# Splitting the gated projection and gates of a hybrid decoder layer into high and low parts, with x kept in DRAM meanwhile

## The chip, the core and the metric

The kernel runs on one core of a Trainium2 chip. The metric is the time of one execution in device microseconds (us). A core has five engines with a queue of instructions each: TensorE (PE, matrix products), VectorE (DVE), ScalarE (ACT), GpSimd (POOL) and SyncE (SP, which here only starts transfers). They meet only through semaphores: an instruction waits for a count, and another one raises it when it is done.

## The reference, cut to what matters

One layer for two groups of tokens that share the weights: 512 prompt tokens and 64 sample tokens (8 sequences of 8), 1024 channels wide.

```python
x = x + 0.5 * swiglu_ffn(rms_norm(x, g_ffn1), w_ffn1_in, w_ffn1_out)
h = rms_norm(x, g_mix)
a_glu, b_glu, q, k, v, qi, ki, wi, gc, ga = split(h @ w_in)
u = a_glu * sigmoid(b_glu)                       # gated projection
q, k = rope(rms_norm(q, g_q)), rope(rms_norm(k, g_k))
scores = sum_h wi * relu(qi . ki);  idx = top_k(scores)   # keys per query
att = softmax(q . k[idx] / 8) @ v[idx]
conv = silu(layer_norm(depthwise_conv31(u))) @ w_cout
x = x + (sigmoid(gc) * conv + sigmoid(ga) * (att @ w_aout)) @ w_o
x = x + 0.5 * swiglu_ffn(rms_norm(x, g_ffn2), w_ffn2_in, w_ffn2_out)
```

Sample tokens gather 256 keys and values each from paged caches of 4096 tokens; prompt tokens attend to keys of the prompt under a mask. q, k, v and the indexer's columns are the "native" part of `h @ w_in`; a_glu, b_glu (512 columns each) and the gates gc, ga (1024 each) are the gated projection and the gates.

## The kernel before

Everything of one token lies in one column: x (`xT`), h (`h32`) and the gates are tiles of 128 channels by 576 tokens (64 sample, 512 prompt), eight of them for 1024 channels. A matmul takes a 128x128 piece of weights and half of the tokens (288).

The program is written out by hand, engine by engine, in the order in which each runs it. In time the stages are: the sample path, the first FFN and the index scores to about 600 us; the native projection to 723.6; `mix_unit` n = 0 to 13 (L1079), PE's gated projection (n = 0 to 7) and the first gate units, to about 869; 32 steps of prompt attention (four blocks of 128 queries times eight heads), into which PE weaves `gate_half`, halves of the units n = 14 to 23 (L1198, in the steps of `HALF_AT`); from `conv_sums` (L1241, about 1063) the norm of the convolution, the output projections (`unit`, L592) and the second FFN.

**Two ways to multiply.** A *fp32 unit* is a weight tile of 128 x 4 x 256 (512 KB) times four tiles of h: 16 matmuls of type fp32, which the profile records as 32 PE records. A *split unit* has its weight in `w_raw` (two slots), from which ACT copies the high part into `w_hi` (L1303, type fp32r) and POOL or DVE subtracts it for the low part `w_lo` (L2651, L1812, L1856); then PE does three products per tile, high by high, high by low, low by high: 48 records. Before, n = 0 to 23 are fp32 units, with weights in a ring of six slots, `wn`, which lies on the place of `w_raw`, `w_hi` and `w_lo`. The output units UM and following are split ones.

**What runs beside.** DVE: `key_logits` (L2356 product, L2359 reduction), one per sample token, 64 in all, 15 of them ("late keys") after the prompt scores; `prompt_qk(0)` and `(1)` (squares, root on ACT, scale, gain, rope) for q and k of the prompt; `u_pair(0)`, `(1)` (gate times projection; they wait for units 3 and 7); the sample softmax over L (64x2560: add bias L2472, maximum L2477, subtract L2478, ACT's Exp L1610, sum L2481, multiply L2483); `choose(b, from, to)`, rounds of eight maxima (L2439, L2440) that pick the prompt's keys per block; `own_heads(0)` (L2508), which waits for PE's first eight value groups. In step i it makes the mask (L2495), four convolution taps (L2530) and the quotient (L2501). POOL gathers key rows (`gather`, L2707, two instructions a token), after the last key clears `zq` and gathers value rows (`gather_values(j)`, L2719, four instructions, 32 groups in three buffers), which PE multiplies in `values(j)` (L1094). SP sends query rows (L476) between weight loads. PE's `logits_turn` (L1113) follows unit 4 and waits for the last key; `probs_turn` (L1121) waits for the normalised L. x stays in `xT`, 2.4 MB, which the final parts read.

## Time and profile before

| | |
|---|---|
| median of 3 runs | 1585.39 us (1580.94 to 1587.18) |
| profiled execution, its own time | 1588.44 us |
| its span in the trace | 1586.6 us |
| PE busy | 1484.6 us, 94% |
| DVE busy | 1104.5 us, 70% |
| POOL busy | 585.4 us, 37% |
| ACT busy | 499.6 us, 31% |

Busy is the time in which an instruction runs; a wait in a queue isn't. "Idle before" in a row names what the instruction was seen to wait for: "issue" is nothing that the profile shows, "remote" something outside of the engines. All times below are from the start of the span.

### The profile page before, as it was taken

To read this page: it belongs to the slowest core of one execution; us is meant where nothing else is said; L and a number is where in the kernel's file an instruction comes from. 1 tells how busy PE (TensorE), PEld (TensorE's weight loads), DVE (VectorE), ACT (ScalarE), POOL (GpSimd) and SP (SyncE) were. 2 spreads that over 40 slices of the span, in tenths; PEclk is the share of its full clock that TensorE was granted. 3 is DMA by queue.
4 is the path that set the end of the run, shared out by engine and by line. 5 is a ranking of instruction groups with operands and counts; after the bars stand their busy time and mean duration, and the time that the engine had idled before them with its cause. 6 is when DMAs were issued, how large, how long until landed. Compare 5 with 4: busy or idle time off the path is not lost. (4 is left out here: it accounts for less than half of the span.)

```text
span 1586.6 us, 20793 instructions
## 1 busy us (share of the span) xinstructions
PE 1484.6 (94%) x8219; PEld 1147.5 (72%) x8219; DVE 1104.5 (70%) x1680; ACT 499.6 (31%) x756; POOL 585.4 (37%) x412
## 2 busy tenths in 40 slices
PE   5989999899999989999899789999999999999998
PEld 2323488677888865446666445669999999999998
DVE  1357399999985898999996676565679865565221
ACT  2233322112112222121212344464346544453221
POOL 2001264443338865554245775013120645520000
PEclk9998999999999999999999898999999999999999
DMA  9994153222226888868458776023422332222222
GB/s 343 389 381 161 50 85 113 93 80 80 80 80 221 286 276 276 290 213 278 125 163 269 222 237 187 17 101 126 138 75 68 93 107 82 92 68 74 74 87 93
DMA packets 156931, 248.77 MB, mean 157 GB/s; under 512 B 11965, under 2 KB 104909, under 8 KB 156571
## 3 DMA queue, kind: packets, MB, share of 16 engines
q1 hardware_dynamic: 131742, 164.22, 32.0%
q0 software_dynamic: 23104, 76.16, 15.4%
q10 hardware_dynamic: 1989, 7.07, 1.1%
q8 instruction: 64, 1.05, 0.3%
q14 instruction: 32, 0.26, 0.0%
HBM read 237.58 MB, written 10.20 MB: 156 GB/s over the span
## 5 line engine op out<-in xcount | busy, mean ns | idle before, releaser
L2651 POOL TENSOR_TENSOR w_lo<-w_raw,w_hi 128x1024 fp32r<-128x1024 f32 x65 | 165.5, 2546 | 294.8 <-ACT w_hi L1303 294.6
L686 PE MATMUL ps<-bh,wqr 128*128 128x288 f32 x936 | 205.3, 295 | 4.2 <-DVE wqr L1843 2.0
L1303 ACT ACTIVATE w_hi<-w_raw 128x1024 fp32r<-128x1024 f32 x88 | 91.5, 1040 | 314.7 <-PE ps L637 231.5
L2707 POOL DMA_INDIRECT kv<-cache_k,idxT x128 | 142.2, 1111 | 81.4 <-DVE kprod L2356 48.9
L2719 POOL DMA_INDIRECT kv<-cache_v,idxT x128 | 134.7, 1052 | 99.3 <-PE ps L1094 47.0
L686 PEld LDWEIGHTS ps<-bh,wqr 128*128 128x128 f32 x936 | 155.5, 188 | 5.0 <-DVE wqr L1843 3.9
L637 PE MATMUL ps<-h_hi,w_hi 128*128 128x512 f32 x352 | 139.2, 395 | 2.8 <-POOL w_lo L2651 1.5
L637 PE MATMUL ps<-h_lo,w_hi 128*128 128x512 f32 x352 | 137.7, 391 | 0.0
L637 PE MATMUL ps<-h_hi,w_lo 128*128 128x512 f32 x352 | 137.7, 391 | 0.0
L1079 PE MATMUL ps<-h,wn 128*128 128x288 f32 x448 | 115.5, 417 | 8.1 <-ACT sgb L1587 4.6
L702 PE MATMUL ps<-a_hi,wqr 128*128 128x288 f32 x704 | 122.3, 295 | 0.0
L686 PE MATMUL ps<-bl,wqr 128*128 128x288 f32 x384 | 113.3, 295 | 0.0
L1079 PEld LDWEIGHTS ps<-h,wn 128*128 128x128 f32 x448 | 86.2, 195 | 37.0 <-ACT sgb L1587 6.2
L1044 PE MATMUL ps<-wn,xg 128*128 128x512 f32 (+1 forms) x256 | 103.2, 563 | 5.0 <-DVE xT L2175 3.0
L702 PEld LDWEIGHTS ps<-a_hi,wqr 128*128 128x128 f32 x704 | 103.1, 188 | 0.0
L1856 DVE TENSOR_TENSOR wqr<-wq,wqr 128x1024 fp32r<-128x1024 f32 (+1 forms) x24 | 27.2, 1135 | 95.2 <-ACT wqr L1341 95.2
L1044 PEld LDWEIGHTS ps<-wn,xg 128*128 128x128 f32 x256 | 49.7, 196 | 56.2 <-issue 47.1
L1198 PE MATMUL ps<-h,wn 128*128 128x288 f32 x320 | 88.3, 432 | 0.7 <-ACT sgb L1686 0.7
L2356 DVE TENSOR_TENSOR kprod<-kv,qb 128x1024 f32<-128x1024 f32 x64 | 81.9, 1280 | 8.5 <-issue 3.1
L2775 POOL TENSOR_TENSOR wq<-wq 128x1024 f32<-128x1024 f32 x10 | 24.9, 2490 | 170.4 <-PE ps L686 76.7
L637 PE MATMUL ps<-a1h,w_hi 128*128 128x512 f32 x176 | 71.6, 407 | 14.8 <-DVE w_lo L1812 7.5
L1198 PEld LDWEIGHTS ps<-h,wn 128*128 128x128 f32 x320 | 62.6, 201 | 27.2 <-issue 8.7
(493 smaller groups left out, 3268.9 us busy)
## 6 DMA issues: line engine op xcount, KB each, us to landing
w_raw<-w_ffn_in SPq DMA_DIRECT2D x56, 512.0 KB, 13.1
wq<-w_ffn_in SPq DMA_DIRECT2D x40, 512.0 KB, 3.6
wn<-w_in SPq DMA_DIRECT2D x36, 512.0 KB
qb<-q_scratch SPq DMA_DIRECT2D x64, 256.0 KB
ring<-w_ffn_in SPq DMA_DIRECT2D x28, 512.0 KB
w_raw<-w_ffn_out SPq DMA_DIRECT2D x24, 512.0 KB, 10.1
wq<-w_ffn_out SPq DMA_DIRECT2D x20, 512.0 KB
ring<-w_ffn_out SPq DMA_DIRECT2D x14, 512.0 KB
```

What stands on the lines that cost most here:

```text
L637: mm = pe.matmul(ps[:, 2 * half + m, :], w[:, k, m * P:(m + 1) * P], x[:, kc0 + k, c0:c0 + SEQ], start=(first and k == 0 and fst), stop=(l ...
L686: mm = pe.matmul(ps[:, bank + m, 0:HALF], w[:, k, m * P:(m + 1) * P], b[:, j, k, :], start=(j in (0, 1, 5) and k == 0 and fst), stop=(k == ...
L702: mm = pe.matmul(ps[:, 4 * half + 2 * m + hf_, 0:HALF], w[:, k, m * P:(m + 1) * P], x[:, kc0 + k, hf_ * HALF:(hf_ + 1) * HALF], start=(kc0 ...
L1044: mm = pe.matmul(ps[:, s % 8, 0:n], xg[:, kk, P * b:P * b + P], wt[:, k, :], start=(kk == 0), stop=(kk == KD - 1))
L1079: mm = pe.matmul(ps[:, 4 * half + 2 * m + hf_, 0:HALF], wt[:, k, m * P:(m + 1) * P], h32[:, 4 * (n % 2) + k, hf_ * HALF:(hf_ + 1) * HALF], ...
L1198: mm = pe.matmul(ps[:, 2 * m + hf_, 0:HALF], wt[:, k, m * P:(m + 1) * P], h32[:, 4 * (n % 2) + k, hf_ * HALF:(hf_ + 1) * HALF], start=(n % ...
L1303: act.activation(w_hi[:, slot, 0:n], w_raw[:, slot, 0:n], ACT.Copy).then_inc(S_("hi_ready"), 1)
L1856: dve.tensor_tensor(wqr[:, 6 + o % 2, 0:n], wq[:, 8 + o % 2, 0:n], wqr[:, 4 + o % 2, 0:n].bitcast(F32), ALU.subtract).then_inc(S_("lo_read ...
L2356: dve.tensor_tensor(kprod[:, :, :], kv[:, n % KV, :, :], qb[:, j, :].unsqueeze(1).to_broadcast([P, 2, DA]), ALU.mult)\
L2651: pool.tensor_tensor(w_lo[:, slot, 0:n], w_raw[:, slot, 0:n], w_hi[:, slot, 0:n].bitcast(F32), ALU.subtract)\
L2707: pool.indirect_dma_start(kv[:, n % KV, c, :], None, rows[0], bass.IndirectOffsetOnAxis(ap=idxT[:, c, n:n + 1], axis=0))\
L2719: pool.indirect_dma_start(kv[:, V_SLOT[j % 3] + a // 2, a % 2, :], None, rows[1], bass.IndirectOffsetOnAxis(ap=idxT[:, j % 2, t:t + 1], ax ...
```

## The change

- All 24 units n = 0 to 23 (now UA + n) become split units, with `x_hi` (eight ACT copies of h, in the place of `xT`) and `h_lo` (eight DVE subtractions ahead of the late keys). ACT makes all high parts; the low parts are made by POOL for n = 0 to 9 and 11, by DVE (`gate_lo`) for 10, 12 to 15 and, in the steps of `HI_AT` (one step later), for 16 to 23.
- x goes to DRAM (`x_scratch`, eight stores by SP at native loads 6 to 8) and comes back, two transfers ahead of each of the loads UM + 4 to UM + 7; DVE waits for it before the first update.
- Raw tiles UA, UA + 1 are loaded once 11 and 14 native loads are used up; the last query rows are sent behind the loads of UA to UA + 3.
- DVE has less to do: the squares of `prompt_qk` are made by ACT (Square over 128x2048) and reduced in one instruction; rope has six instructions and not seven; the subtraction and the sum of the softmax are gone, ACT's Exp is eight instructions with a bias and an accumulated sum; `choose(1, 7, 16)` and `choose(2, 0, 2)` follow `u_pair(1)`.
- `probs_turn` follows unit 7, the stores of k and v are waited for at gate unit 6 and not 10, and SP, ACT and POOL lose waits for `ring_used` ahead of UM's loads.

```diff
-        UM = UA
+        UM = UA + 24
+        HI_AT = {3: 16, 5: 17, 9: 18, 11: 19, 15: 20, 17: 21, 21: 22, 25: 23}
...
+                if m < NB + 2:
+                    sp.wait_ge(S_("ring_used"), N_RING + (11, 14)[m - NB])
+                load(UA + m - NB, win_v[:, 4 * (m % 2):4 * (m % 2) + 4, col:col + 256], m % 2, 1024)
+                while m < NB + 4 and sent[0] < (55, 57, 60, NS)[m - NB]:
+                    query_load(sent[0])
+                    sent[0] += 1
...
+                unit(UA + n, n % 2, x_hi, h_lo, 4 * (n % 2), 4, half, n % 2 == 0, n % 2 == 1, between)
...
-                if n == 6:
+                if n == 7:
                     probs_turn()
...
+                    act.wait_ge(S_("nat_evac"), 8)
+                    act.activation(qk_sq[:, :, :], qn[:, :, :], ACT.Square).then_inc(S_("nat_squares"), 1)
                     for j in range(3):
                         relu(8 * j, 8 * j + 8)
+                        if j < 2:
+                            act.wait_ge(S_("x_moved"), 64 + 16 * KD)
+                            for k in range(4 * j, 4 * j + 4):
+                                act.wait_ge(S_("hf_ready"), KD + k + 1)
+                                act.activation(x_hi[:, k, :], h32[:, k, :], ACT.Copy).then_inc(S_("hhi_ready"), 1)
...
-            act.activation(L[:, :, :], L[:, :, :], ACT.Exp, scale=HD ** -0.5).then_inc(S_("exp_ready"), 1)
+            for h in range(H):
+                act.activation(L[:, h, :], L[:, h, :], ACT.Exp, scale=HD ** -0.5, bias=small[0:NS, 40 + h:41 + h],
+                               accum_out=small[0:NS, 50 + h:51 + h]).then_inc(S_("exp_ready"), 1)
...
+            for k in range(KD):
+                dve.wait_ge(S_("hhi_ready"), KD + 1 + k + 1)
+                dve.tensor_tensor(h_lo[:, k, :], h32[:, k, :], x_hi[:, k, :].bitcast(F32), ALU.subtract).then_inc(S_("h_ready"), 1)
...
+            def gate_lo(n):
+
+                dve.wait_ge(S_("lo_ready"), UA + n + 2)
+                split_lo(UA + n, n % 2)
...
             while sent[0] < NS:
+                if sent[0] == 56:
+                    pool.wait_ge(S_("ring_used"), N_RING + 13)
+                    lo(UA)
+                if sent[0] == 62:
+                    pool.wait_ge(S_("ring_used"), N_RING + NB)
+                    lo(UA + 1)
                 gather()
+            lo(UA + 2)
             pool.wait_ge(S_("logits_ready"), NS + 1)
             pool.memset(zq[:, :, :, :], 0.0).then_inc(S_("zq_zero"), 1)
-            pool.wait_ge(S_("ring_used"), N_RING + NB + 3)
-            for j in range(3):
-                gather_values(j)
+            gather_values(0)
+            lo(UA + 3)
+            lo(UA + 4)
+            gather_values(1)
+            lo(UA + 5)
+            gather_values(2)
+            lo(UA + 6)
             pool.wait_ge(S_("shift_ready"), 1)
             pool.memset(zq2[:, :, :, :], 0.0).then_inc(S_("zq_zero"), 1)
+            for n in range(7, 10):
+                lo(UA + n)
             for j in range(3, 32):
+                if j == 5:
+                    pool.wait_ge(S_("lo_ready"), UA + 11 + 2)
+                    lo(UA + 11)
                 gather_values(j)
```

The order on POOL around the last key (kv is the buffer of gathered rows). Before:

```order
L2707 DMA kv<-cache_k,idxT 128x512 [waits kv_used]
L2707 DMA kv<-cache_k,idxT 128x512
L2744 MEMSET zq 128x448 [waits logits_ready]
L2719 DMA kv<-cache_v,idxT 128x512 [waits kv_used,ring_used]
L2719 DMA kv<-cache_v,idxT 128x512 x3
L2719 DMA kv<-cache_v,idxT 128x512 [waits kv_used]
L2719 DMA kv<-cache_v,idxT 128x512 x3
```

And now, from the split of unit 1 on:

```order
L2705 TENSOR_TENSOR w_lo<-w_raw,w_hi 128x1024 [waits hi_ready,ring_used]
L2761 DMA kv<-cache_k,idxT 128x512 [waits kv_used]
L2761 DMA kv<-cache_k,idxT 128x512
L2761 DMA kv<-cache_k,idxT 128x512 [waits kv_used]
L2761 DMA kv<-cache_k,idxT 128x512
L2705 TENSOR_TENSOR w_lo<-w_raw,w_hi 128x1024 [waits hi_ready]
L2805 MEMSET zq 128x448 [waits logits_ready]
L2773 DMA kv<-cache_v,idxT 128x512 [waits kv_used]
L2773 DMA kv<-cache_v,idxT 128x512 x3
L2705 TENSOR_TENSOR w_lo<-w_raw,w_hi 128x1024 [waits hi_ready] x2
L2773 DMA kv<-cache_v,idxT 128x512 [waits kv_used]
L2773 DMA kv<-cache_v,idxT 128x512 x3
```

The splits of units 0 and 1 stand among the last key gathers, that of unit 2 ahead of the wait for the last key (logits_ready), those of units 3 and 4 behind the first group of values.

On DVE, the end of the sample softmax (L is the tile of logits, sgb the sigmoid, m_192 and m_194 the eight maxima of a round of `choose`). Before:

```order
L2439 MAX m_192<-bias_new 128x8 [waits dve_own]
L2440 MATCH_REPLACE bias_new<-m_192,bias_new 128x256 [waits dve_own]
L2481 TENSOR_REDUCE small<-L 64x8 [waits exp_ready,dve_own]
L2482 RECIPROCAL small<-small 64x8 [waits dve_own]
L2483 TENSOR_TENSOR L<-L,small 64x2560 [waits dve_own]
L2439 MAX m_192<-bias_new 128x8 [waits dve_own]
L2440 MATCH_REPLACE bias_new<-m_192,bias_new 128x256 [waits dve_own]
```

And now:

```order
L2474 MAX m_194<-bias_new 128x8 [waits dve_own]
L2475 MATCH_REPLACE bias_new<-m_194,bias_new 128x256 [waits dve_own]
L2520 RECIPROCAL small<-small 64x8 [waits exp_ready,dve_own]
L2521 TENSOR_TENSOR L<-L,small 64x2560 [waits dve_own]
L2220 TENSOR_TENSOR U_s<-sgb,ps 128x8x8 [waits unit_used,mix_free,sgb_ready]
L2222 TENSOR_TENSOR U_p<-sgb,ps 128x224
L2223 TENSOR_TENSOR U_p<-sgb,ps 128x288
```

The sum is gone, and `u_pair(1)` (L2220 to L2223) has moved ahead of the rounds that stood behind the product.

On DVE, a step of the prompt attention (Lp the masked logits, yacc the convolution's sum). Before:

```order
L2495 ISA Lp,small<-ps,causal 128x128 [waits plog_done]
L2495 ISA small 128x1
L2530 SCALAR_TENSOR_TENSOR yacc<-U_p,wconv,yacc 128x512 [waits dve_own]
L2530 SCALAR_TENSOR_TENSOR yacc<-U_p,wconv,yacc 128x512 x3
L2501 RECIPROCAL small<-small 128x1 [waits pexp_ready]
```

And now, in a step that follows one of `HI_AT`:

```order
L2541 ISA Lp,small<-ps,causal 128x128 [waits plog_done]
L2541 ISA small 128x1
L2580 SCALAR_TENSOR_TENSOR yacc<-U_p,wconv,yacc 128x512 [waits dve_own]
L2580 SCALAR_TENSOR_TENSOR yacc<-U_p,wconv,yacc 128x512 x3
L1849 TENSOR_TENSOR w_lo<-w_raw,w_hi 128x1024 [waits hi_ready,lo_ready]
L2547 RECIPROCAL small<-small 128x1 [waits exp_ready]
```

A split stands between the taps and the quotient, with a wait for ACT's high part.

## Rows read from the trace of the kernel before

**Rows 1.** Windows: us, busy of PE, PEld, DVE, ACT, POOL, clock, DMA.
```profile
724.00:798.00 74.00, 67.84 (x298) 52.55 (x297) 69.09 (x106) 13.88 (x17) 19.53 (x17) 0.98 0.54 168
798.00:869.00 71.00, 66.14 (x329) 43.42 (x327) 54.35 (x100) 14.40 (x32) 36.78 (x37) 0.98 0.70 220
869.00:998.00 129.00, 113.32 (x527) 64.78 (x527) 88.26 (x175) 50.09 (x119) 82.40 (x80) 0.92 0.68 208
844.30:850.00 5.70, 5.69 (x16) 4.02 (x16) 0.00 (x0) 1.28 (x3) 2.89 (x4) 0.70 0.97 332
```

**Rows 2.** Timeline of DVE: start, us, line, operation, count, idle before.
```profile
740.00 1.22 DVE L2359 TENSOR_REDUCE G<-kprod 128x16 f32<-128x1024 f32 x1
...
781.46 2.82 DVE L2483 TENSOR_TENSOR L<-L,small 64x2560 f32<-64x2560 f32 x1
...
795.86 0.22 DVE L2185 TENSOR_TENSOR U_s<-sgb,ps 128x64 f32<-128x64 f32 x1
...
797.57 1.22 DVE L2081 TENSOR_TENSOR rt<-kn 128x1024 f32<-128x1024 f32 x1
...
851.24 0.69 DVE L2508 TENSOR_TENSOR mz<-ps,headmask 128x512 f32<-128x512 f32 x1 [13.97 <-issue]
...
873.46 0.27 DVE L2495 CUSTOM_DVE_ANT_0 Lp<-ps,causal 128x128 f32<-128x128 f32 x1
```

**Rows 3.** Timeline of PE, late units and the first steps.
```profile
821.78 4.15 PE L1079 MATMUL ps<-h,wn 128*128 128x288 f32 x16
...
844.31 5.81 PE L1079 MATMUL ps<-h,wn 128*128 128x288 f32 x16 [2.99 <-ACT sgb L1587]
...
874.39 0.49 PE L1213 MATMUL ps<-kTp,qTp 64*128 64x128 f32 x2
877.75 1.32 PE L1094 MATMUL ps<-kv,zq 128*32 128x512 f32 x8 [2.87 <-issue]
```

**Rows 4.** Timeline of PE, fp32 units, the logits' turn, and a split unit.
```profile
723.64 14.71 PE L1079 MATMUL ps<-h,wn 128*128 128x288 f32 x60
...
762.44 1.91 PE L1113 MATMUL ps<-ident,G 128*64 128x128 f32 x16
...
1067.72 0.53 PE L592 MATMUL ps<-t_hi,w_hi 128*128 128x288 f32 x2 [0.16 <-DVE t_lo L2582]
...
1074.17 4.04 PE L1241 MATMUL ps<-ysq,ones 128*128 128x288 f32 x16
```

**Rows 5.** Groups by line, DVE from 1063 to 1068 us (busy, mean ns).
```profile
L2582 DVE TENSOR_TENSOR t_lo<-attT,t_hi 128x576 fp32r<-128x576 f32 x4 | 2.8, 752 | 6.2 <-ACT t_hi L1742 6.2
```

**Rows 6.** Timeline of ACT at the native projection and the softmax.
```profile
718.69 0.69 ACT L1583 ACTIVATE vnp<-ps,small 128x512 f32<-128x512 f32 x1 [16.61 <-issue]
...
774.65 2.34 ACT L1610 ACTIVATE L<-L 64x2560 f32<-64x2560 f32 x1
```

**Rows 7.** Timelines of POOL and of DVE at an earlier POOL split.
```profile
496.20 2.40 POOL L2651 TENSOR_TENSOR w_lo<-w_raw,w_hi 128x1024 fp32r<-128x1024 f32 x1
...
496.63 3.04 DVE L2356 TENSOR_TENSOR kprod<-kv,qb 128x1024 f32<-128x1024 f32 x1
```

**Rows 8.** Timeline of POOL after the last key.
```profile
741.28 0.47 POOL L2744 MEMSET zq<- 128x448 f32 x1 [13.56 <-DVE G L2359]
747.36 3.00 POOL L2719 DMA_INDIRECT kv<-cache_v,idxT  x1 [5.60 <-PE ps L1079]
750.66 2.01 POOL L2719 DMA_INDIRECT kv<-cache_v,idxT  x1 [0.30 <-issue]
752.98 0.95 POOL L2719 DMA_INDIRECT kv<-cache_v,idxT  x1 [0.30 <-issue]
```

**Rows 9.** The page's groups of instructions: busy, mean ns, idle before.
```profile
L1303 ACT ACTIVATE w_hi<-w_raw 128x1024 fp32r<-128x1024 f32 x88 | 91.5, 1040 | 314.7 <-PE ps L637 231.5
...
L702 PEld LDWEIGHTS ps<-a_hi,wqr 128*128 128x128 f32 x704 | 103.1, 188 | 0.0
L1856 DVE TENSOR_TENSOR wqr<-wq,wqr 128x1024 fp32r<-128x1024 f32 (+1 forms) x24 | 27.2, 1135 | 95.2 <-ACT wqr L1341 95.2
```

145 lines of the change are left out of this document (86 added, 59 removed).

## The prediction

> **What bounds the kernel now.** I read the table of windows first, then the timelines of DVE and PE, and last POOL's. [rows 1] is that table. From 724 to 869 us PE is busy for 134 of 145 us, DVE for 123; from 869 to 998 us, where the prompt attention runs in steps, PE has 113.3 and DVE 88.3 of 129. So PE leads by little, and DVE is second. The timelines show where the two take turns: DVE ends the last key of the sample logits at 741.2, works on `prompt_qk`, softmax and `choose`, waits 13.97 us for PE's sparse values up to 851.24, and makes its first prompt mask at 873.46 [rows 2]; PE comes to step 1 at 874.39, so both reach the steps together [rows 3]. Whatever either engine is given or spared before 873 counts only by what the later one of the two does. After the steps nothing of the program changes but the reload of x; that stretch (from `conv_sums` on) I move as a block.
>
> **What the split saves on PE.** A gated unit is 32 fp32 records: 14.71 us for 60 of them is 0.245 each, 7.8 us a unit. The same tile shape in high and low parts is 48 records; those of the first output unit start at 1067.72 and the next thing starts at 1074.17: 6.45 us [rows 4]. That is 1.36 us a unit, 0.68 a half, and 33 us for the 24 units if all of it were on the path.
>
> **What is added ahead of the first unit.** DVE makes h_lo, eight subtractions of 128x576, between the prompt scores and the last fifteen keys. Four such keep DVE busy for 2.8 us [rows 5], so 5.5 us. ACT's first Square of 128x2048 and its eight x_hi copies stand ahead of relus whose scores DVE waits for; an Exp of 2560 columns took ACT 2.34 us [rows 6], so the Square takes about 1.9. What of this DVE feels the trace can't show; I take 1.0, with ends 0 (ACT has idle time) and 3. Then POOL's splits of units 0 to 2 run beside the keys. The trace shows what that costs: while POOL split from 496.20 to 498.60, DVE's product of keys took 3.04 us and not 1.22, ending where it would if it had begun when the split ended [rows 7]. The next two such collisions cost less, since a split may begin under the reduction, which is not held up. I take 1.2 each, 3.7 for three (ends 0 and 7). The Trainium skill, "SBUF — State Buffer", section "SBUF: two separate sides", says that VectorE's operation with two SBUF inputs and a GpSimd operation reading SBUF exclude each other for the whole instruction; by it the POOL splits are no free cover, and without it the sum would be about 4.5 us lower. The trace agrees. Last key: 741.2 + 5.5 + 1.0 + 3.7 = **751.4**.
>
> **The new wait.** Splits of units 0 to 2 stand ahead of POOL's wait for the last key, but the split of unit 3 stands behind it, behind a memset (0.47) and behind `gather_values(0)`. Before, the first two gathers of values took 3.00 and 2.01 us beside DVE's 2048-wide products, the later ones 0.95 with 0.30 between [rows 8]: 8.1 us for the four, 5.0 without such neighbours. A split takes 2.4 [rows 7], and may stand behind one more DVE product: 751.4 + 0.5 + 8.3 + 0.8 + 2.4 = 763.4. PE began unit 0 at 723.64 [rows 4]; 1.0 later and with three units of 6.45 it is free at 744. It **waits about 19 us** for unit 3. All of PE's saving up to here and 15 us more is gone; behind the wait stand units 3 to 7, the logits' turn, and by these DVE's softmax and `u_pair(1)`. After 2.99 us of idleness a half took 5.81 instead of 4.15 us [rows 3, 4], in a window with a granted clock of 0.70 [rows 1], that is, part of it at the lower level of 1.2 GHz; I add 1.7. Five units at 6.45, the turn (1.9 [rows 4]) and 1.7 make 35.9: PE ends unit 7 at 799.3, and `u_pair(1)`, 1.7 us from 795.86 to 797.57 [rows 2], ends at **801.0** where it ended at 797.57. DVE's removed work (two passes over L of 2.8 us each, and the first `prompt_qk`'s squares) lies in this stretch. It buys nothing, since DVE waits for unit 7 anyway; nor does the longer Exp on ACT cost anything: 2.34 us in eight pieces [rows 6], say 6 with what each piece adds, against the 12 us that PE still needs for units 6 and 7.
>
> **DVE from there to the first mask.** Before: 873.46 − 797.57 = 75.9, less the wait of 13.97 and 0.3: 61.6 of work. Added: the `choose` rounds that stood between 784.28 and 795.86 and now follow `u_pair(1)`, 11.6 [rows 2]; five `gate_lo` of 1.14 [rows 9], 5.7. Taken off in `prompt_qk(1)`: squares in four passes of 1.22 [rows 2] become one reduction over 2048, about 2.2, and the copy of rope goes, 0.7: 3.4. Sum 75.5. The wait of 13.97 is filled: DVE now comes to `own_heads(0)` at about 850, when PE, with units of 6.45 us, has the eighth value group. `gate_lo(13)` waits for an ACT split that waits for unit 11, 2.3 us; one more POOL split (11) collides, 0.5. First mask at 801.0 + 75.5 + 2.8 = 879.3, **+5.8**. PE is through its units at 860 and idles.
>
> **Steps.** Step 1 loses its wait of 2.87 us for a V gather [rows 3], since POOL has had time to run ahead; half of it returns as DVE's own chain there: −1.4. From step 2 on PE is the longer engine: thirteen halves × 0.68 = −8.8; DVE's six `gate_lo` there make a step DVE-bound now and then: +0.6. Steps 21 to 34: six halves, −4.1, and +0.7 for the last two `gate_lo`. Together −8.2 and −3.4. POOL's five us for a value group stay below the steps' 5.6.
>
> The tail is unmoved: x goes out behind native loads while the DMA share is high but nobody waits for these eight, and comes back over 50 us before the first use.
>
> **Sum:** +5.8 − 1.4 − 8.2 − 3.4 = **−7.2**. The profiled run of before took 1588.44, so its like would be 1581.2; the median of the three shown is 1585.39, so **1578.2**. A measurement of this kernel can tell about 0.5%, 7.9 us, from no change; this lies just inside.
>
> **Rivals.**
> (1) *The wait at unit 3 is shorter or is absorbed.* If gathers and splits meet no DVE products, unit 3 starts at 751.4 + 0.5 + 5.0 + 2.4 = 759.3 and without slow restart: 5.8 less, so −13.0, 1572.4. If moreover the keys are not held up, 3.7 less: 1568.7. The end of this side is DVE without any wait: before, DVE took 56.4 us from the last key to the end of `u_pair(1)`, of which it waited about 1.9; without 9.0 of removed work and 11.6 of moved rounds 33.9 are left, and 78.3 behind: 863.6, −9.9 instead of +5.8: 1562.5. For it: the gathers' 0.95 rows; against it: [rows 7, 8].
> (2) *Slower: the chain within a step binds, not PE's sum.* A mask on DVE, exp on ACT, quotient on DVE, scale on ACT, turn on PE. ACT is busy for 50 and DVE for 88 us of the 129 [rows 1], and they wait for each other. Then shorter halves buy nothing, and each step with a split adds 1.04 on ACT and 1.14 on DVE [rows 9]: eight × 2.2 = +17.6 in place of −11.6. With +5.8 − 1.4 it gives +22, 1607; where only half of the steps are so, +7.4, 1592.8. It decides from the point where DVE's and ACT's work of one step exceeds PE's 5.6 us. Against it: PE's 113 of the same 129 us.
> (3) *The split gives nothing.* Each record needs a weight load of 0.188 [rows 9]; were these not hidden, a unit would be 9.0 us. Against it stand the 6.45 us of rows 4. +29 and more: 1614.
> (4) *Gathers 56 to 63 come late*, behind the splits of units 0 and 1 on POOL: the last key moves one for one once the split of unit 0 ends after 721. ACT, which makes the high parts, idled 16.61 us before 718.69 [rows 6], so this is unlikely; I give it no more than a part of the slower chance, at 1586 to 1594.
>
> **Chances.** Forecast, −7.9 to +7.9: 0.44. Rival 1, beyond −7.9: 0.41. Rivals 2 and 4, beyond +7.9: 0.12; rival 3: 0.03. Faster 0.41, same 0.44, slower 0.15. The range of 8 in 10 takes rival 1 to its end, and of rival 2 the half: 1562.5 to 1592. The forecast's own range is 1572 to 1586.
>
> **What would show it.** PE's unit 3 starts at 763 after a wait of 15 to 20 us put down to POOL's w_lo; if it starts before 755 the POOL reasoning is wrong. 48 records a unit in 6.45 us. DVE's key product near a POOL split at 2 to 3 us. The first mask at 876 to 882, with PE idle for over 10 us before it. Steps from first mask to `conv_sums` 12 to 14 us shorter. If instead DVE's idle time in steps shrinks and PE's grows, rival 2 holds. Wrong altogether: waits for x or for query rows in the profile.

## The result, and the profile after

| | before | after |
|---|---|---|
| median of nine runs each, first chip | 1585.39 us | 1591.68 us |
| ratio, 95% interval | | 1.0038 [1.0019, 1.0056] |
| profiled execution, its span | 1586.6 us | 1589.6 us |
| PE busy | 1484.6 us | 1456.8 us |
| DVE busy | 1104.5 us | 1123.6 us |
| POOL busy | 585.4 us | 624.2 us |

The change made the kernel slower by 6.3 us of median, which is small but outside of the interval. Two more comparisons on other chips gave 1.0051 [1.0032, 1.0071] and 1.0066 [1.0044, 1.0087]. The forecast had been 7.2 us faster; the time lies 0.3 us inside the upper end of the range. PE lost 27.8 us of work, of the 33 that the prediction gave for all 24 units, and none of it reached the end.

Where the time went, as distances between marks that both traces have (c0 is one more trace of the kernel before, c1 and c2 are two more of the kernel after, on other chips; c0 and c1 share one):

| us | before | c0 | after | c1 | c2 | forecast for after |
|---|---|---|---|---|---|---|
| end of the last key | 741.2 | 743.6 | 756.0 | 755.5 | 757.4 | 751.4 |
| end of `u_pair(1)` | 797.6 | 799.9 | 806.5 | 805.8 | 807.1 | 801.0 |
| first prompt mask | 873.5 | 875.8 | 891.0 | 894.2 | 893.0 | 879.3 |
| first mask to that of step 20 | 118.6 | 118.7 | 110.4 | 109.7 | 108.3 | 109.0 |
| mask of step 20 to `conv_sums` | 71.3 | 71.1 | 64.9 | 67.9 | 67.7 | 67.9 |
| `conv_sums` | 1063.4 | 1065.6 | 1066.3 | 1071.8 | 1069.1 | 1056.2 |
| from there to the end of the span | 523.2 | 524.2 | 523.3 | 523.9 | 523.2 | unmoved |

So the steps shortened just as forecast, and the first mask came 12 us later than forecast. Read like this, the failure would lie wholly ahead of the first mask. The experiments speak against this reading: where the first mask came early, the steps did not shorten.

These marks come from one profiled execution each. That of the kernel before took 1588.44 us, 3 us more than its median, so in the first pair `conv_sums` moved by only 2.9 us, and by 6.2 from c0 to c1.

Windows of the kernel after, against [rows 1] (us, busy of PE, PEld, DVE, ACT, POOL with counts, clock, DMA share, GB/s):

```profile
724.00:869.00 145.00, 116.61 (x825) 103.08 (x824) 122.36 (x174) 45.73 (x78) 95.61 (x70) 0.91 0.63 200
869.00:998.00 129.00, 103.36 (x624) 69.13 (x624) 107.69 (x205) 56.51 (x124) 88.62 (x83) 0.88 0.71 216
998.00:1061.00 63.00, 60.79 (x383) 45.35 (x382) 45.97 (x91) 35.84 (x67) 2.39 (x1) 0.95 0.18 62
```

In the middle window PE fell by 10.0 us against [rows 1], DVE rose by 19.4 and POOL by 6.2: the three longest now have 103, 108 and 89 of 129. POOL's number leaves out the 0.30 us for which it is idle after each gather, about 80 times in that window; with them POOL is taken for some 113 of the 129 us.

Timeline of the kernel after on DVE, from the low parts of h to the first mask (start, us, line, operation, idle before):

```profile
706.23 5.43 DVE L2500 TENSOR_TENSOR h_lo<-h,x_hi 128x576 fp32r<-128x576 f32 x8
...
716.80 2.90 DVE L2391 TENSOR_TENSOR kprod<-kv,qb 128x1024 f32<-128x1024 f32 x1
...
736.77 1.91 DVE L2391 TENSOR_TENSOR kprod<-kv,qb 128x1024 f32<-128x1024 f32 x1
...
743.55 3.34 DVE L2391 TENSOR_TENSOR kprod<-kv,qb 128x1024 f32<-128x1024 f32 x1 [1.00 <-DMA qb<-q_scratch]
...
754.76 1.22 DVE L2394 TENSOR_REDUCE G<-kprod 128x16 f32<-128x1024 f32 x1
...
784.06 3.11 DVE L2510 COPY L<-nlog 64x512 f32<-64x512 f32 x1 [3.50 <-PE ps L1119]
...
828.19 3.41 DVE L2097 TENSOR_TENSOR rt<-kn,ropetp 128x1024 f32<-128x1024 f32 x1
...
848.98 1.26 DVE L1849 TENSOR_TENSOR w_lo<-w_raw,w_hi 128x1024 fp32r<-128x1024 f32 x1 [3.76 <-ACT w_hi L1311]
...
864.08 1.23 DVE L1849 TENSOR_TENSOR w_lo<-w_raw,w_hi 128x1024 fp32r<-128x1024 f32 x1 [2.91 <-issue]
...
891.00 0.28 DVE L2541 CUSTOM_DVE_ANT_0 Lp<-ps,causal 128x128 f32<-128x128 f32 x1
```

The eight subtractions took 5.43 us, forecast 5.5. A key product beside a POOL split took 2.90, 1.91 and 3.34 us. The last reduction ends at 755.98.

The new wait, on POOL's timeline of the kernel after:

```profile
743.40 2.40 POOL L2705 TENSOR_TENSOR w_lo<-w_raw,w_hi 128x1024 fp32r<-128x1024 f32 x1
...
756.04 0.47 POOL L2805 MEMSET zq<- 128x448 f32 x1 [10.24 <-DVE G L2394]
...
759.19 2.99 POOL L2773 DMA_INDIRECT kv<-cache_v,idxT  x1 [0.30 <-issue]
...
764.53 5.93 POOL L2705 TENSOR_TENSOR w_lo<-w_raw,w_hi 128x1024 fp32r<-128x1024 f32 x2
```

and on PE's:

```profile
767.20 0.85 PE L608 MATMUL ps<-x_hi,w_hi 128*128 128x288 f32 x2 [14.64 <-POOL w_lo L2705]
...
782.04 1.91 PE L1119 MATMUL ps<-ident,G 128*64 128x128 f32 x16
```

PE waits 14.64 us for the split of unit 3, put down to POOL's `w_lo` as forecast; the forecast had 19 us, since it let PE begin unit 0 at 724.6, and PE began it at 728.2 and waited 2.62 us for the split of unit 1. Windows of the kernel after (columns as above), of unit 8 and then of the two units behind the wait:

```profile
806.50:813.10 6.60, 6.58 (x49) 6.41 (x49) 6.15 (x21) 3.92 (x6) 2.06 (x1) 1.00 0.34 101
```

```profile
767.20:774.90 7.70, 7.70 (x43) 7.70 (x44) 7.63 (x5) 0.00 (x0) 6.94 (x4) 0.71 0.65 182
774.90:782.00 7.10, 7.10 (x55) 7.10 (x54) 4.75 (x17) 1.06 (x1) 6.25 (x5) 1.00 0.71 206
```

The first row is unit 8: 48 records of it, and one more, in 6.6 us with the granted clock at 1.00, forecast 6.45 for a unit. After 14.64 us of idleness the clock is 0.71 for 7.7 us, part of it at 1.2 GHz, and 43 records fill them, where the next 7.1 us at 1.00 hold 55.

### The profile page after: what moved, and what is told of

It reads as the page before. It is cut to its first block and busy times, and to the rows that moved or that the text cites. A ratio compares the mean times of both kernels' runs of the same rounds, so it can differ in the third digit from the quotient of the medians.

```text
span 1589.6 us, 21713 instructions
## 1 busy us (share of the span) xinstructions
PE 1456.8 (92%) x8603; PEld 1162.9 (73%) x8603; DVE 1123.6 (71%) x1687; ACT 533.9 (34%) x805; POOL 624.2 (39%) x423
## 5 line engine op out<-in xcount | busy, mean ns | idle before, releaser
L2705 POOL TENSOR_TENSOR w_lo<-w_raw,w_hi 128x1024 fp32r<-128x1024 f32 x76 | 194.6, 2561 | 294.1 <-ACT w_hi L1311 293.8
L1311 ACT ACTIVATE w_hi<-w_raw 128x1024 fp32r<-128x1024 f32 x112 | 116.9, 1044 | 367.7 <-PE ps L653 235.3
L2773 POOL DMA_INDIRECT kv<-cache_v,idxT x128 | 142.7, 1114 | 62.5 <-issue 35.0
L2391 DVE TENSOR_TENSOR kprod<-kv,qb 128x1024 f32<-128x1024 f32 x64 | 86.6, 1353 | 13.7 <-DMA qb<-q_scratch 5.8
L653 PE MATMUL ps<-a1h,w_hi 128*128 128x512 f32 x176 | 71.1, 404 | 15.3 <-DVE w_lo L1849 8.0
L2580 DVE SCALAR_TENSOR_TENSOR yacc<-U_p,wconv,yacc 128x512 f32<-128x512 f32 x116 | 81.4, 763 | 0.0
L1880 DVE TENSOR_TENSOR wqr<-wq,wqr 128x1024 fp32r<-128x1024 f32 x47 | 74.8, 1604 | 7.8 <-ACT wqr L1334 6.0
L653 PEld LDWEIGHTS ps<-h_hi,w_hi 128*128 128x128 f32 x352 | 66.7, 189 | 18.0 <-issue 2.1
L2394 DVE TENSOR_REDUCE G<-kprod 128x16 f32<-128x1024 f32 x64 | 78.2, 1222 | 2.2
```

Of the source, the lines that this page charges most:

```text
L653: mm = pe.matmul(ps[:, 2 * half + m, :], w[:, k, m * P:(m + 1) * P], x[:, kc0 + k, c0:c0 + SEQ], start=(first and k == 0 and fst), stop=(l ...
L1311: act.activation(w_hi[:, slot, 0:n], w_raw[:, slot, 0:n], ACT.Copy).then_inc(S_("hi_ready"), 1)
L1880: dve.tensor_tensor(wqr[:, s, :], wq[:, s, :], left_hi(i, j).bitcast(F32), ALU.subtract).then_inc(S_("lo_ready"), 1)
L2391: dve.tensor_tensor(kprod[:, :, :], kv[:, n % KV, :, :], qb[:, j, :].unsqueeze(1).to_broadcast([P, 2, DA]), ALU.mult)\
L2394: dve.tensor_reduce(G[:, :, n], kprod[:, :, :].rearrange("p c (h d) -> p (c h) d", h=H), AX.X, ALU.add).then_inc(S_("logits_ready"), 1)
L2580: link(dve.scalar_tensor_tensor(out=yacc[:, k, NS:NT], in0=U_p[:, k, j:j + SEQ], scalar=wj, in1=yacc[:, k, NS:NT], op0=ALU.mult, op1=ALU.add))
```

## Experiments

Ratios are to the kernel before on the same chip. Chips differ: the kernel before had a median of 1568 to 1588 us on them, so times of different groups of runs are compared as ratios only. The kernel after had 1.0038, 1.0051 and 1.0066 on the three chips on which it ran unchanged; a difference of 0.2% between ratios from two chips says nothing.

### Group 1: the parts ahead of the first mask

The four ran on one chip, and the kernel after didn't run there unchanged.

**DVE's savings alone**, in the kernel before:

```diff
-            act.activation(L[:, :, :], L[:, :, :], ACT.Exp, scale=HD ** -0.5).then_inc(S_("exp_ready"), 1)
+            for h in range(H):
+                act.activation(L[:, h, :], L[:, h, :], ACT.Exp, scale=HD ** -0.5, bias=small[0:NS, 40 + h:41 + h],
+                               accum_out=small[0:NS, 50 + h:51 + h]).then_inc(S_("exp_ready"), 1)
...
-                qk_squares(v, rt1[:, :, :, :].rearrange("p b h d -> p (b h) d"), msq, rt2[:, 0, 0:1, :].rearrange("p a b -> p (a b)"))\
-                    .then_inc(S_("ms_ready"), 1)
+                lk(dve.tensor_reduce(msq, qk_sq[:, :, :].rearrange("p b (h d) -> p (b h) d", d=HD), AX.X, ALU.add))
```

> The kernel before with only the savings on VectorE: squares by ACT and one reduction, six rope instructions, no subtraction and no sum in the sample softmax, eight Exp with bias and accumulated sum. The places of choose and u_pair stay. Chain theory: of the 12.6 us removed from DVE only what stands between the logits' turn and the probabilities' turn is on the path, since PE is waited for elsewhere (the 13.97 us before 851.24): probabilities' turn 3 us earlier (784.3 to 781), first mask 3 us earlier, the whole 3 us faster, about 1582.4. Rival, DVE binds from the last key to the first mask: 10 to 12 us faster, about 1574. Second rival, it comes to nothing because ACT's Square delays the scores: 0.

1.0008 [0.9994, 1.0022]. The savings are worth nothing alone, as the prediction said of the softmax part ("it buys nothing, since DVE waits for unit 7 anyway"). The first mask stands at 869.9, `conv_sums` at 1047.0. Since its time is that of before, this trace serves below as the one of before for this chip; its profiled execution took 1571.48 us, 3.4 more than the median of the kernel before there.

**The split of unit 3 ahead of POOL's wait for the last key**, in the kernel after:

```diff
             lo(UA + 2)
+            lo(UA + 3)
             pool.wait_ge(S_("logits_ready"), NS + 1)
...
             gather_values(0)
-            lo(UA + 3)
             lo(UA + 4)
```

> The changed kernel with one line moved: POOL makes the low part of unit 3 before it waits for the last key, not after it and behind the first group of values. Chain theory (last key, POOL, unit 3, units 4 to 7, u_pair(1), first mask): unit 3 starts at 752 to 756 and not at 767.2; the last key comes 2 us later because one more key product is held up by a POOL split; the logits' turn, now waiting for u_pair(0), comes at 777 and not at 782; first mask and end 5 us earlier than in the changed kernel, about 1587. Rival, DVE's own work between last key and first mask binds and the wait of PE at unit 3 only shows idle time: 0 to 2 us, about 1591.

1.0052 [1.0033, 1.0071]. PE's timeline in that kernel:

```profile
766.09 0.82 PE L608 MATMUL ps<-x_hi,w_hi 128*128 128x288 f32 x2 [9.46 <-POOL w_lo L2705]
```

The wait has only moved on: unit 3 starts in time, unit 4 now waits 9.46 us for a split that stands behind the gathers. The logits' turn came at 774.4, the first mask at 882.5, `conv_sums` at 1050.5, and the ratio is among those of the kernel after.

**No subtraction on POOL** (w_lo of all gated units that POOL splits is filled with zeros by a memset):

```diff
-                split_lo(u, u % 2, usize(u))
+                if UA <= u < UM:
+                    pool.wait_ge(S_("hi_ready"), u + 1)
+                    pool.memset(w_lo[:, u % 2, :].bitcast(F32), 0.0).then_inc(S_("lo_ready"), 1)
+                else:
+                    split_lo(u, u % 2, usize(u))
```

> The changed kernel in which POOL's low parts of the gated units are set to zero by a memset in place of the subtraction (the low parts of 11 units are left out; same semaphores). A memset reads nothing from SBUF. Lock theory (a POOL subtraction holds up DVE's products): no key product over 1.3 us, last key 4.5 us earlier (756 to 751.5), rope instructions and the copy of new logits back at 1.2 and 0.4 us, unit 3 about 7 us earlier, first mask 10 us earlier (891 to 881), time about 1582. Rival, POOL's own duration is what counts and DVE isn't held up by it: only the 1.3 us less for the split of unit 3, 2 us in all, about 1590.

1.0016 [1.0001, 1.0031]. DVE's groups by line between the scores and the last key, first of the kernel after (704 to 757 us), then of this one (704 to 760), each with busy, mean ns of one, and idle before:

```profile
L2391 DVE TENSOR_TENSOR kprod<-kv,qb 128x1024 f32<-128x1024 f32 x16 | 24.1, 1503 | 2.7 <-DMA qb<-q_scratch 1.0
```

```profile
L2391 DVE TENSOR_TENSOR kprod<-kv,qb 128x1024 f32<-128x1024 f32 x15 | 18.4, 1225 | 2.3 <-DMA qb<-q_scratch 0.5
```

With a memset in its place the split costs DVE nothing: products take 1.225 us, not 1.503. The last key ended at 749.3 and the first mask came at 879.4, which is 11.6 us ahead of the kernel after on the first chip; `conv_sums`, at 1045.3, was ahead of the stand-in for before (1047.0), and the median still 0.16% behind. The edit relieves POOL, too: a memset takes it 0.97 us and a split 2.4. That matters further down, where POOL's gathers of values come up.

**Short h_lo** (16 of 576 columns subtracted, x_hi in its place in the products):

```diff
-                dve.tensor_tensor(h_lo[:, k, :], h32[:, k, :], x_hi[:, k, :].bitcast(F32), ALU.subtract).then_inc(S_("h_ready"), 1)
+                dve.tensor_tensor(h_lo[:, k, 0:16], h32[:, k, 0:16], x_hi[:, k, 0:16].bitcast(F32), ALU.subtract).then_inc(S_("h_ready"), 1)
```

> The changed kernel in which DVE subtracts only 16 of 576 columns for each of the eight h_lo tiles and PE takes the high part of h in its place (the product of high weights and low h is left out in value, not in work). Chain theory: the 5.4 us come off one for one: last key 751, first mask 886, end 5 us earlier, about 1587. Rival, something else is late at the keys (query rows, gathers, POOL): the last key moves by less than 2.5 us and so does the end.

1.0056 [1.0037, 1.0076]; last key at 752.4, first mask at 885.4, `conv_sums` at 1051.5. Taking 4.6 us off DVE there didn't show in the time.

What follows from the four: the early split and the short h_lo leave the ratio where the kernel after has it, though each takes some us off the way to the first mask. Only the memset brought something, 5.0 us of median against the short h_lo, with a first mask 6.1 us earlier. This alone would fit a first mask that counts one for one. But its gathers moved as well: the last gather of values ends at 980.2 for 986.4, as much earlier as `conv_sums` (1045.3 for 1051.5). Which of the two counts, the next groups tell.

### Group 2: the steps, with the first mask early

**Nine rounds of choose(3) moved into the steps** (nobody needs them before step 24), so that the first mask is no longer late:

```diff
+        CHOOSE_AT = (0, 2, 8, 14, 17, 19, 20, 21, 22)
...
-            choose(3, 6, 16)
+            choose(3, 6, 7)
...
+                if i in CHOOSE_AT:
+                    r = 7 + CHOOSE_AT.index(i)
+                    choose(3, r, r + 1)
```

> The changed kernel with nine of the sixteen rounds of choose for the last block of queries (1.52 us each on DVE) moved from ahead of the first mask into steps 0, 2, 8, 14, 17 and 19 to 22, of which none has a low part or, up to 16, a sample convolution. The block's mask is first needed in step 24. Theory, DVE's work binds the first mask while PE idles 13 us before it: first mask 13 us earlier, steps 21 to 24 a little longer, end 8 to 11 us earlier than in the changed kernel. Rival, PE's late units bind the steps and DVE's lateness costs only idle time: 0 to 3 us. Second rival, the steps' chains take it back: first mask 13 us earlier, conv_sums within 3 us of the changed kernel.

1.0055 [1.0036, 1.0074], against 1.0051 [1.0032, 1.0071] of the kernel after, unchanged, on the same chip:

> The changed kernel, unchanged, on the chip of the next two. Expected by the first comparison: 0.2 to 0.6% slower than before. If the wait at unit 3 and the first mask (17 us late in the first pair) are the same here while the 13 to 15 us won in the steps shrink, as the steps of the experiments above suggest (177 and 168 us), it is 0.6 to 0.9% slower.

and the kernel before:

> The kernel before, unchanged, for a trace from the same chip as the next three. The chain of after is compared against it mark by mark. Expected: last key at about 741, first mask 873, conv_sums at the place of the first trace or up to 15 us earlier, since the kernels of the first group of experiments ran 17 us faster on their chip than the kernels on the first one.

The masks of steps 0 and 20 on DVE, in c0, c1 and this kernel:

```profile
875.83 0.28 DVE L2495 CUSTOM_DVE_ANT_0 Lp<-ps,causal 128x128 f32<-128x128 f32 x1
...
994.50 0.54 DVE L2495 CUSTOM_DVE_ANT_0 Lp<-ps,bias_new 128x384 f32<-128x384 f32 x1
```

```profile
894.20 0.28 DVE L2541 CUSTOM_DVE_ANT_0 Lp<-ps,causal 128x128 f32<-128x128 f32 x1
...
1003.94 0.54 DVE L2541 CUSTOM_DVE_ANT_0 Lp<-ps,bias_new 128x384 f32<-128x384 f32 x1
```

```profile
877.20 0.29 DVE L2542 CUSTOM_DVE_ANT_0 Lp<-ps,causal 128x128 f32<-128x128 f32 x1 [0.23 <-DVE bias_new L2476]
...
996.86 0.56 DVE L2542 CUSTOM_DVE_ANT_0 Lp<-ps,bias_new 128x384 f32<-128x384 f32 x1
```

The first mask came 17.0 us earlier and the mask of step 20 only 7.1. From the one to the other it took 118.7, 109.7 and 119.7 us. Six of the nine rounds lie between these two masks and bring DVE 8.7 us (96.5 us busy for 87.9 in c1), into a stretch in which DVE had waited for others. So with the first mask in its old place the steps take as long as before, though their halves are split: the shortening of 8 to 10 us in the steps of the kernel after was not won by the split units. By this run alone it could be the moved rounds that took it back, if DVE paced the steps; the run with half of the taps, in the next group, speaks against that.

PE in this kernel waits early in the steps for nothing that the profile names, ahead of the products of gathered values:

```profile
884.09 1.93 PE L1101 MATMUL ps<-kv,zq 128*32 128x512 f32 x8 [6.04 <-issue]
```

**All known losses mended** (the former, with the split of unit 3 early, ACT's first Square behind the relus, and `gate_lo(13)`, `(14)` three rounds later):

```diff
+            lo(UA + 3)
             pool.wait_ge(S_("logits_ready"), NS + 1)
...
-            choose(2, 2, 8)
+            choose(2, 2, 11)
             gate_lo(13)
-            choose(2, 8, 16)
+            choose(2, 11, 16)
             own_heads(0)
+            choose(3, 0, 3)
             gate_lo(14)
```

> The same with three things more: unit 3's low part ahead of the wait for the last key, ACT's first Square behind the relus of the prompt scores, and the low parts of units 13 and 14 three rounds of choose later, where the trace of the changed kernel shows DVE waiting 3.8 and 2.9 us for ACT's high part. Chain theory: to the 10 us of the run before come 5 for unit 3, 2 for the Square, up to 5 for the waits, of which PE's own late units will swallow half: 14 to 18 us faster than the changed kernel, 7 to 12 us faster than before. Rival: no more than 3 us beyond the run before, since PE, not DVE, then binds the start of the steps.

1.0050 [1.0031, 1.0069]: first mask at 875.0, before the one of c0, `conv_sums` at 1067.5, still 1.9 us behind it. So a first mask in time, 0.9 us ahead of c0's, does not bring the time of before back.

### Group 3: which engine paces the steps

Three engines came into question for steps 2 to 20: PE, DVE with the masks and taps, and POOL with four gathers of values per group. Each was relieved alone. ACT, with its part of the softmax in each step, was not.

This group ran on a chip as quick as that of group 1 (a median of 1569 and 1568 us for the kernel before), and its base, the kernel with moved rounds, wasn't traced there. From the first mask to that of step 20 the stand-in for before took 105.9 us in group 1, where the kernel before took 118.6 and 118.7 on slower chips. The distances below must be set beside each other and beside that 105.9, and not beside the 119.7 of group 2.

**Half of the gathers from group 15 on** (the former with moved rounds as base; two of four gathers left out):

```diff
+                    if j >= 15 and a == 1:
+                        break
```

> The kernel with nine rounds of choose in the steps (first mask early, no gain at the end), in which POOL issues only two of the four value gathers of each group from the 15th on (the other two quarters of those groups are left out, PE multiplies what the buffer held). Theory A, POOL's gathers pace steps 2 to 20: from the first mask to the 20th 119.7 us become about 100, the end 12 to 20 us earlier, 0.990 to 0.995 of before. Theory B, the chain mask, Exp, quotient, scale, turn through DVE, ACT and PE paces the steps: less than 4 us.

The counts that PE waits for are lowered to match. 1.0038 [1.0020, 1.0055], for 1.0055 of its base on another chip; masks at 879.1 and 982.9, 103.9 apart, in the slowest of its nine executions. POOL now waits for PE, here at its last gathers:

```profile
961.96 0.94 POOL L2777 DMA_INDIRECT kv<-cache_v,idxT  x1 [3.38 <-PE ps L1101]
963.21 0.95 POOL L2777 DMA_INDIRECT kv<-cache_v,idxT  x1 [0.30 <-issue]
967.97 0.95 POOL L2777 DMA_INDIRECT kv<-cache_v,idxT  x1 [3.82 <-PE ps L1101]
```

**Half of the convolution's taps on DVE** (same base):

```diff
-                for k in range(KC):
+                for k in range(KC if j in (0, CW - 1) else 2):
```

> The same kernel as its base, in which DVE makes the taps of the convolution for two of four channel tiles only (half of that work is left out): 1.4 us less of DVE in every step. Theory B, DVE's part of the chain paces the steps: steps 2 to 20 shorter by 1.0 to 1.4 us each, 20 us or more, and steps 21 to 31 as well. Theory A, POOL's gathers: DVE gives way, but the gathers still come at 6 us a group: less than 6 us up to step 20.

1.0063 [1.0044, 1.0083], from four runs; masks at 873.9 and 982.2, 108.3 apart. DVE is busy for 73.4 us between them, less than the 80.7 of the kernel before, and the steps are no shorter for it. So it isn't DVE's moved rounds that keep the steps long. In the table of waits from 880 to 998 us (engine, line waited for, us in total, times, longest) DVE now waits for PE's scores:

```profile
DVE Lp L2542 <- PE ps L1222: 31.5, 14, 4.6
```

**Half of the matmuls in the gate halves, kernel before** (38 us of PE's work gone):

```diff
-                for k in range(4):
+                for k in range(2):
...
-                                       start=(n % 2 == 0 and k == 0), stop=(n % 2 == 1 and k == 3))
+                                       start=(n % 2 == 0 and k == 0), stop=(n % 2 == 1 and k == 1))
```

> The kernel before, in which PE does only half of the matmuls of each gate half in the steps (the other half of the channels is left out): 2 us less of PE in each of 20 steps, three times what the split saves. My prediction held PE for the longer engine there: then the 13 halves of steps 2 to 20 give 26 us and the six later ones 12, the time about 0.977 of before. Rival, PE's time is cover and gathers or the softmax chain pace the steps: less than 8 us in steps 2 to 20, 0.99 or more.

0.9926 [0.9903, 0.9948]: 12 to 13 us won for 38 removed. Its table of waits from 880 to 998 us:

```profile
PE ps L1094 <- DMA kv<-cache_v,idxT: 16.3, 9, 3.6
```

and its last gather of values on POOL, and the mask of step 20 on DVE:

```profile
969.07 0.95 POOL L2719 DMA_INDIRECT kv<-cache_v,idxT  x1 [0.30 <-issue]
```

```profile
971.78 0.53 DVE L2495 CUSTOM_DVE_ANT_0 Lp<-ps,bias_new 128x384 f32<-128x384 f32 x1
```

The windows from the first mask to that of step 20 (columns as above), of the stand-in for before and then of this kernel:

```profile
869.92:975.85 105.93, 99.06 (x479) 56.82 (x479) 80.67 (x160) 48.11 (x113) 80.57 (x76) 0.95 0.76 239
```

```profile
868.14:971.78 103.64, 83.10 (x378) 41.56 (x375) 80.50 (x159) 47.81 (x113) 79.03 (x76) 0.85 0.79 244
```

There are 101 records fewer, 24.7 us of work at 0.245 each, and the stretch is 2.3 us shorter. PE's busy time fell by 16.0 us only, with the granted clock at 0.85 for 0.95, and its idle time rose from 6.9 to 20.5 us. From the mask of step 20 to `conv_sums` it took 57.2 against 71.2: 56 records fewer, 13.7 us of work, gave 14.0. So **PE alone sets the pace behind step 20, and not before it.** In the stretch before it PE, spared, waits for gathered values, and the last gather is issued less than 3 us ahead of the mask of step 20.

**The store of x shortened** (kernel after; 8 of 576 columns per transfer, to see whether the transfer holds up the scores):

```diff
-                        sp.dma_start(x_dram[:, k, :], xT[:, k, :]).then_inc(S_("x_moved"), 16)
+                        sp.dma_start(x_dram[:, k, 0:8], xT[:, k, 0:8]).then_inc(S_("x_moved"), 16)
...
-                    sp.dma_start(xT[:, k, :], x_dram[:, k, :]).then_inc(S_("x_moved"), 16)
+                    sp.dma_start(xT[:, k, :], inp["w_o"].rearrange("o (k p) n -> p (o k) n", p=P)[:, k, 0:NT]).then_inc(S_("x_moved"), 16)
```

> The changed kernel in which x isn't stored: 8 of 576 columns go out per tile, and the same number of bytes comes back from another tensor (x is left out of the result's sum). ACT's x_hi copies wait for these stores, and relus of the prompt scores stand behind the copies. Theory, the 4 us by which the scores end later than before (706.2 for 702.1) come of that wait: h_lo begins 3 to 4 us earlier, first mask 3 us earlier, end 2 to 3 us earlier. Rival, the lateness is ACT's own Square and copies (1.9 + 8 x 0.7 us): less than 1 us.

```profile
700.66 5.43 DVE L2500 TENSOR_TENSOR h_lo<-h,x_hi 128x576 fp32r<-128x576 f32 x8
```

h_lo started at 700.7; with the whole store it started at 703.2 and 708.3 in the two other traces of this chip, and between 703.9 and 709.5 on the others. So at least 2.5 us of the late scores are the store of x, which the prediction had at nothing; more can't be said with traces 5 us apart. The time, 1.0084 [1.0059, 1.0108], is no better, so this edit, too, moved a mark and not the end (its median rests on four runs).

Its first mask stands at 885.2 and that of step 20 at 983.9. The kernel with half of the taps, on the same chip, has 873.9 and 982.2: of a first mask 11.3 us earlier, 1.8 us are left at step 20.

### Groups 4 and 5: the chain of value gathers

What remained was POOL's chain: 29 groups of four gathers from group 3 on, each at least 4 x 1.25 = 5.0 us, 145 together, begun when PE has used value group 0. POOL's timeline at group 3 and at the last gather, of the kernels before and after:

```profile
806.92 2.21 POOL L2719 DMA_INDIRECT kv<-cache_v,idxT  x1 [31.85 <-PE ps L1094]
...
983.69 0.95 POOL L2719 DMA_INDIRECT kv<-cache_v,idxT  x1 [0.30 <-issue]
```

```profile
814.47 0.97 POOL L2773 DMA_INDIRECT kv<-cache_v,idxT  x1 [5.91 <-PE ps L1100]
...
827.86 2.66 POOL L2705 TENSOR_TENSOR w_lo<-w_raw,w_hi 128x1024 fp32r<-128x1024 f32 x1
...
995.92 0.94 POOL L2773 DMA_INDIRECT kv<-cache_v,idxT  x1 [0.30 <-issue]
```

and POOL's gathers by line from 805 to 1000 us, before and after (busy, mean ns, idle before):

```profile
L2719 POOL DMA_INDIRECT kv<-cache_v,idxT x116 | 119.2, 1027 | 90.4 <-PE ps L1094 47.0 <-issue 31.6 <-remote 11.8
```

```profile
L2773 POOL DMA_INDIRECT kv<-cache_v,idxT x116 | 126.3, 1089 | 59.3 <-issue 31.8 <-PE ps L1100 17.9 <-remote 9.6
```

The last gather ends at 984.6 before and 996.9 after. These rows sum to it: before 806.9 + 119.2 + (90.4 − 31.85); after 814.5 + 126.3 + 2.7 for the split of unit 11 + (59.3 − 5.91). Of the 12.2 us between them **7.5 are the later start, 7.1 longer gathers, 2.7 the split in the chain, and −5.1 fewer waits.** From c0 to c1 the start is 4.5 us later and the end 10.2, so the shares vary from trace to trace. The longer ones stand where DVE has wide instructions (2.99 us at 759.19); that DVE's added subtractions make them so is argued, not tried apart.

**Start earlier, no split in the chain** (kernel after; values(0) between the halves of unit 8, unit 11 split by DVE):

```diff
-        V_AFTER = {8: (0, 1), 9: (2,), 10: (4,), 11: (6,), 13: (9, 10)}
-        V_WITHIN = {10: 3, 11: 5, 12: 7, 13: 8}
+        V_AFTER = {8: (1,), 9: (2,), 10: (4,), 11: (6,), 13: (9, 10)}
+        V_WITHIN = {8: 0, 10: 3, 11: 5, 12: 7, 13: 8}
...
-            prompt_qk(1)
+            prompt_qk(1, lambda: gate_lo(11))
...
-                if j == 5:
-                    pool.wait_ge(S_("lo_ready"), UA + 11 + 2)
-                    lo(UA + 11)
```

> The changed kernel with two moves that shorten GpSimd's chain of value gathers and nothing else: PE multiplies the first value group between the halves of unit 8 and not after it (3.3 us earlier, so gather group 3 starts at 810 for 814), and the low part of unit 11 is made by DVE inside prompt_qk(1) and not by GpSimd between groups 4 and 5 (2.7 us less there, 1.2 more on DVE but one collision of 2.2 less). First mask stays late (within 2 us of the changed kernel). Gather theory: last value gather 5 to 6 us earlier, step 20 and the end 4 to 5 us earlier than the changed kernel. Rival, DVE's late first mask carries the loss: end within 1.5 us of the changed kernel.

1.0022 [1.0009, 1.0034], where the kernel after had, on this chip, 1.0066:

> The changed kernel, unchanged, as the measure for the three others of this group. 1.004 to 1.009 of before. Steps: the 20th mask within 5 us after the last value gather.

```profile
809.99 0.97 POOL L2775 DMA_INDIRECT kv<-cache_v,idxT  x1 [2.71 <-PE ps L1100]
...
987.92 0.95 POOL L2775 DMA_INDIRECT kv<-cache_v,idxT  x1 [0.30 <-issue]
```

5.6 us faster than the kernel after, with the chain's start 5.1 us earlier than c2's (815.11) and its end 9.3 earlier. One part of the expectation failed: the first mask moved too, from 893.0 to 885.8, since DVE no longer meets the split of unit 11 inside the rope. So this run alone doesn't tell chain from mask. That a first mask 17 us earlier by itself brought nothing (group 2) speaks for the chain.

**Both chains mended** (the kernel with all known losses mended, plus this edit):

> The kernel with everything mended on the DVE side (choose rounds in the steps, unit 3's low part early, Square late, splits 13 and 14 later) with the same two moves. It gave 0.9999 of the changed kernel's ratio without them. Gather theory: now both chains are shorter, last gather at least 8 us earlier than in the changed kernel, end 7 to 10 us earlier: 0.999 to 1.001 of before. Rival, a third thing (transfers, the softmax chain of each step) paces the steps: no more than 3 us from the changed kernel.

1.0007 [0.9995, 1.0020]: as fast as the kernel before. First mask at 866.0, `conv_sums` at 1058.6. In group 2, on another chip, the same mending without the edit on the gathers gave 1.0050, with its first mask at 875.0. Against the kernel after on the same chip the former gained 0.6%, the latter nothing, and the first mask was early in both.

**The same in the kernel before**, first with DVE's savings, then with nothing else; the second differs from the kernel before by where one call stands:

```diff
-        V_AFTER = {8: (0, 1), 9: (2,), 10: (4,), 11: (6,), 13: (9, 10)}
-        V_WITHIN = {10: 3, 11: 5, 12: 7, 13: 8}
+        V_AFTER = {8: (1,), 9: (2,), 10: (4,), 11: (6,), 13: (9, 10)}
+        V_WITHIN = {8: 0, 10: 3, 11: 5, 12: 7, 13: 8}
```

> The kernel before with the DVE savings and the first value group multiplied between the halves of unit 8. Gather theory: group 3 is gathered 3.5 to 4 us earlier, step 20 comes 2 to 4 us earlier, 0.997 to 0.999 of before. Rival, PE's own work binds (fp32 units): 0 to 1 us, 1.000 to 1.001.

> The kernel before, with the first value group multiplied between the halves of unit 8 and not after it, and nothing else. Gather theory: group 3 is gathered 3.5 to 4 us earlier (805 for 809), step 20 comes 2 to 3 us earlier, 0.998 to 0.999 of before. Rival, what e13 won was won by the DVE savings: 0.9995 to 1.0005.

0.9976 [0.9959, 0.9994] and **0.9958 [0.9941, 0.9975]**, on two chips. The second is 6.1 us faster than the kernel before (1579.51 against 1585.66 us): with the first, whose interval overlaps, the fastest of the kernels that leave nothing out, and it has no split gates at all. Its chain, in the slowest of its seven executions (1584.65 us):

```profile
805.63 0.95 POOL L2719 DMA_INDIRECT kv<-cache_v,idxT  x1 [29.43 <-PE ps L1094]
...
978.24 0.95 POOL L2719 DMA_INDIRECT kv<-cache_v,idxT  x1 [0.30 <-issue]
```

**Start later alone** (kernel before; POOL waits ahead of group 3 until PE has used three groups):

```diff
+            pool.wait_ge(S_("pv_used"), 3)
             for j in range(3, 32):
```

> The kernel before, in which GpSimd waits for the third value product, after unit 9, ahead of gather group 3, and nothing else: group 3 comes at about 817 for 809. Gather theory: the chain has 29 groups of at least 5.0 us behind it and little slack, so last value gather and step 20 come 4 to 8 us later, 1.003 to 1.005 of before; that is what the changed kernel does to the chain. Rival, the chain has slack: less than 2 us.

1.0045 [1.0028, 1.0061]: 1593.34 us, 7.7 us slower, by nothing but a wait ahead of the gathers.

```profile
816.79 0.95 POOL L2719 DMA_INDIRECT kv<-cache_v,idxT  x1 [41.67 <-PE ps L1094]
...
986.23 0.94 POOL L2719 DMA_INDIRECT kv<-cache_v,idxT  x1 [0.30 <-issue]
```

This is the size of the whole change's loss, made in the kernel before without touching PE, DVE or ACT. The trace doesn't show how: group 3 starts 9.9 us later than before, the first mask comes 3.5 us later (876.9), and the last gather ends only 2.5 us later, with `conv_sums` at 1063.4 as before. The profiled execution took 1587.8 us, at the low end of this kernel's runs (1585.5 to 1597.7), so the loss that the median has isn't in it.

## Why the prediction was wrong

In short: the prediction took less work on PE for shorter steps. Up to step 20 PE doesn't set their length alone, so its saving bought nothing there; POOL's gathers of values, which the change started later and slowed, came in as one more pacemaker.

**Right.** The first mask waited for DVE, with PE idle for 12.95 us before it, as forecast. A split unit in 6.6 us for 6.45; h_lo 5.43 for 5.5; POOL's splits hold up DVE's products (2.90, 1.91 and 3.34 us for 1.22), in sum 4.5 us for the 3.7 forecast; PE waits for the split of unit 3, put down to POOL's `w_lo`; nothing moves behind `conv_sums`; DVE's savings buy nothing by themselves. The lock is the one that the Trainium skill, "SBUF — State Buffer", section "SBUF: two separate sides", states for an operation with two SBUF inputs beside a GpSimd instruction that reads SBUF; the memset experiment shows it from the other side, and the reduction between the products kept its 1.22 us.

**Mis-sized, ahead of the first mask: +17.5 instead of +5.8.** The terms, in the order of the prediction:
- Last key 756.0, not 751.4. h_lo starts 4.1 us late (706.23 where the scores ended at 702.1 before) and not 1.0: the store of x, taken at nothing, makes up at least 2.5 of it (group 3). The prediction said "nobody waits for these eight" stores, but in the change itself ACT waits for them (`x_moved`) ahead of its x_hi copies, and relus of the prompt scores stand behind those. Whether it is this wait or the transfers' traffic that delays the scores the runs don't tell. The locks took 0.8 more than forecast, and a query row, which was to come in time, 1.0.
- Unit 3 starts 11.2 us after the last key, forecast 12.0. Units 3 to 7 and the turn took 1.5 us more than forecast, of which 1.3 is one more wait of PE between them; what the lower clock cost (14.8 us for two units that take 13.2 at 1.00) is the 1.7 of the forecast, 1.6 measured. `u_pair(1)` ends at 806.5, not 801.0.
- From there to the mask DVE took 84.5 us, not 78.3: 3.76 and 2.91 us of waits for high parts (`gate_lo(13)` and `(14)`, forecast 2.3 for one of them), and a rope product of 3.41 us under the split of unit 11 (forecast 0.5 for it).

These are seven small terms of one sign, and only one, the 0.8 us at unit 3, of the other.

**The step that failed** is "From step 2 on PE is the longer engine: thirteen halves × 0.68 = −8.8", together with "POOL's five us for a value group stay below the steps' 5.6". The number −9.6 for steps 1 to 20 came out (−8.2, −9.0 and −10.4 in the three pairs), for another reason than the one given. With 25 us of PE's work removed, these steps shortened by 2 us (group 3); with the split halves and the first mask early they took 119.7 us for 118.7 (group 2). Several engines are nearly level there: PE with 113 of 129 us, DVE, and POOL with groups of at least 5.0 us that in fact took 6.1 us each before (177.7 us for 29 groups, from the rows above; 5.6 in the stand-in for before on its quicker chip). The prediction compared POOL's *least* time for a group with the step's 5.6, and so took for slack what is full in fact. The last gather is issued 8.4 us ahead of the mask of step 20 before, 5.5 after. So a late first mask is made good in the steps, most likely since the gathers run ahead meanwhile, and an early one is worth next to nothing (group 2 shows the second). It follows that the late first mask, 11.7 us later than forecast, explains the miss in the sum but not in the kernel: with the mask at 877.2, where the forecast had 879.3, `conv_sums` came at 1067.9 (forecast 1056.2, and 1065.6 in the kernel before on that chip).

Distance from the end of the last gather to `conv_sums`, where PE alone sets the pace (as the half gates showed), on the chips of the first comparison and of groups 2, 4 and 5:

| kernel | group 3 starts | last gather ends | `conv_sums` | between | ratio |
|---|---|---|---|---|---|
| before | 806.9 | 984.6 | 1063.4 | 78.8 | 1 |
| before (c0) | 809.3 | 989.3 | 1065.6 | 76.3 | 1 |
| before, values(0) early | 805.6 | 979.2 | 1060.0 | 80.8 | 0.9958 |
| the same with DVE's savings | 802.4 | 980.1 | 1056.2 | 76.1 | 0.9976 |
| before, POOL waits | 816.8 | 987.2 | 1063.4 | 76.2 | 1.0045 |
| after | 814.5 | 996.9 | 1066.3 | 69.4 | 1.0038 |
| after (c1) | 813.8 | 999.5 | 1071.8 | 72.3 | 1.0051 |
| after (c2) | 815.1 | 998.2 | 1069.1 | 70.9 | 1.0066 |
| after, chain mended | 810.0 | 988.9 | 1064.2 | 75.3 | 1.0022 |
| after, moved rounds | 812.9 | 992.9 | 1067.9 | 75.0 | 1.0055 |
| all mended | 812.5 | 994.9 | 1067.5 | 72.6 | 1.0050 |
| both | 807.0 | 985.1 | 1058.6 | 73.5 | 1.0007 |

The kernels with split gates need 69 to 75 us behind the last gather and those without 76 to 81: there the split gives its gain, six halves and what PE still had open. But the kernel after has its last gather 12.2 us later than before in the first pair and 10.2 from c0 to c1, and what the two leave is the 2.9 and 6.2 us at `conv_sums`. The change moved group 3 behind a later probabilities' turn, put a split of 2.7 us into the chain, and its gathers were longer.

**Rivals.** Rival 2 had the sign right and, with half of the steps so, the time (1592.8 forecast, 1591.7 measured). That the number fits is luck: it had the first mask 5.8 us later and the stretch from it to `conv_sums` 1.6 us longer, where the mask came 17.5 later and the stretch was 14.6 shorter. Of its mechanism one part is met: it said that shorter halves buy nothing in the steps, which is so up to step 20, but put it down to DVE's and ACT's chain; the runs show POOL's chain as one more member, which no rival named. Relieving DVE (half of the taps) gave no gain; ACT's part was never tried. Rival 1's "faster" needed the first mask to count one for one, which group 2 disproves, and with the splits' locks gone altogether (group 1) the kernel was still 0.16% behind. Rival 3 is out by the 6.6 us of unit 8; rival 4 by the last key's terms, all of which have other names.

**What stays open.** The gathers alone are no bound either: with half of them left out from group 15 on, the kernel had 1.0038 for the 1.0055 of its base, on different chips and within the two intervals. How the engines share the pace in steps 2 to 20 was not resolved further. Many of the waits there are put down to "remote" or "issue", where several engines stand still together; in the kernel before, from 880 to 998 us:

```profile
DVE Lp L2495 <- remote: 21.8, 8, 5.8
ACT pTp L1708 <- remote: 13.8, 4, 6.0
POOL kv L2719 <- remote: 7.3, 4, 2.0
```

The traces show one thing about them that the study didn't use. All twelve traces from slower chips (a median of 1584 to 1588 us for the kernel before) have such "remote" waits in this window; none of the eight from the two quicker chips (1568 and 1569 us) has a single one. With them the steps up to 20 take 115 to 119 us in kernels without the split and 108 to 110 in the kernel after; without them 105.9 us in the stand-in for before and 99 to 102 in the four close relatives of the kernel after (early split, memset, short h_lo, short store). DVE and ACT are busy equally long in either case (80.7 and 48 us in the kernel before and in its stand-in). So the difference goes with these waits, 7 to 13 us of the steps. That they make it isn't shown, nor what they are, and group 3, on a quicker chip, tested steps without them. In the trace of the kernel with values(0) early, the chain starts 1.3 us earlier than before and ends 5.4 earlier, the difference being shorter waits (53.3 us for 58.5), and the first mask moved by 2.4 us. That the place of the start counts is shown by the times of one edit in each direction; how it comes to be worth more than itself isn't, and the first mask moved with it in both (by 2.4 us one way and 3.5 the other). Nor is it known why chips differ by up to 20 us with one and the same kernel; most of it lies in these steps.

## What to carry to other kernels

Before spending a busy engine's time, ask for each engine in the loop how long its share of one pass *really* takes, with its issue gaps and its waits, and not what it would take at best; an engine with a third of its time idle by the profile's page can still be one of those that set the pace. Where several engines are level, test each by removing a large part of its work from the kernel as it stands: half of the gate matmuls left out would have told, before anything was written, that the split can win only behind step 20. Take base and edit on the same chip. And look where a paced chain *starts*: moving one call by half a unit gave 6 us, as much as the large change lost.

## What the runs showed of the hardware

- A subtraction of 128x1024 on POOL holds up DVE's product with two SBUF inputs by 0.7 to 2.1 us (1.91 to 3.34 for 1.22), and also a copy: the COPY into L at 784.06 took 3.11 us where the same took 0.42 before. It doesn't hold up a reduction. A memset on POOL in its place, 0.97 us long, holds up nothing (1.225 us for each product, also where the two overlap).
- It works the other way, too: to issue a gather takes POOL 0.95 us, and 2 to 3 us beside a wide DVE instruction (2.99 at 759.19). Over 116 gathers the mean went from 1.027 to 1.089 us.
- An indirect gather of 128 rows costs POOL 1.25 us, 0.95 and a gap of 0.30, at the least; in the kernel before a chain of 116 of them takes 178 us, from 806.9 to 984.6, and in its stand-in on a quicker chip 163.
- After 14.64 us of idleness PE's granted clock was 0.71 over the next 7.7 us, part of them at 1.2 GHz, and 1.00 over the 7.1 us after that.
- With 101 matmul records fewer over the same steps, PE's granted clock was 0.85 and not 0.95, and its busy time fell by 16.0 us where the records taken out stand for 24.7.
